# Odd mixer of a three-way-split fp32 transformer step: narrower weight splits, and rotation, gate prelude and first attention scores placed among the projections

## Chip, cores and metric

One core of one Trainium2 chip runs the whole program. The metric is the device time in microseconds of one execution (one core, so this core's time), and the median over repeated executions.

## The reference, cut to what is computed

The program is a stack of layers on 512 tokens of width 1024, all in float32: an even mixer, cross attention, SwiGLU, then the **odd mixer**, cross attention, SwiGLU and two further layers (gated delta rule with a long convolution, with SwiGLU on both sides). The change touches the odd mixer, and the weight splits of every SwiGLU's down projection. The odd mixer is:

```
z = h @ w_in
q_m, k_m, v_m, o_m, gates, c_q, c_kv, k_r = split(z)
i_pre, f_pre = gates + bias                      # 4 heads each
hm = mlstm(q_m, k_m, v_m, i_pre, f_pre)          # decays from cumulative log_sigmoid(f_pre)
hm = rmsnorm(sigmoid(o_m) * hm)
q  = rmsnorm(c_q) @ w_uq    # 8 heads: 64 plain + 32 rotated columns
kv = rmsnorm(c_kv) @ w_ukv  # 8 heads: 64 key + 64 value columns
ha = causal_softmax_attention(q_nope, rope(q_rope), k_nope, rope(k_r), v)
out = concat(hm, ha) @ w_out
```

`w_uq` has 384 rows, `w_ukv` 256, every other weight matrix of the mixer 1024.

## The kernel before, in words

**Linear stages.** `schedule()` gives a list of stages. A linear stage is cut into blocks of 256 output columns; a block fills two banks of the PSUM tile `ACC` (pair 0 or 1, alternating with the running block number). Its weights come in units of 128 x 2048 floats: the SP queue loads `RAW` (two slots), ACT casts it to `WH` (L1836, `split_hi`), DVE forms `WL = RAW - WH` (L2340, `split_lo`), and PE runs three matmuls for each 128x128 tile and 512 tokens (L1003 to L1005: high by high, high by low, low by high). A unit of a matrix with 384 or 256 rows fills 768 or 512 of the 2048 columns, and the third unit of a down projection's block 1536; the load brings only those, the casts of ACT and DVE cover all 2048. The load of unit n waits until unit n-2 is split, `split_hi` of n until PE is through with n-2. DVE then evicts the finished block (L2411 scaled, L2419 plain, L2430 for values, L2435 and L2436 for the two halves of a "nope" block, which go to 64 partitions each).

**The odd mixer's order.** Each engine walks the same list and does its own part in program order; semaphores join them. `od_v` (values of the mLSTM), `od_in` (latents, the rotary key and the gate columns, `OZ[:, 0:6]`), `od_rest` (six blocks: queries, keys, output gates of the mLSTM), into which the latents' norm is already woven (`latent_sums` L1213 after block 2, `latent_scales` L1220 after block 4); `latent` casts the normed latents into `HH` (ACT L2042) and `HL` (DVE L2661); then `uq_nope` (2 blocks), `uq_rope` (1), `kv_nope` (2), `kv_v` (2). The first weight unit of `od_out` is split within the second block of `kv_v`.

**Attention (`mla`, L1680, L2250, L2757).** PE rotates the queries (L1684) and the key (L1685) by a matmul with a fixed matrix, and keeps itself busy with `keep_clock` (13 matmuls on ones, L1010) while DVE multiplies by cosine and sine (L2761 to L2770: three operations for the key, then for each half of the queries two products and four sums of 32 partitions). Then for each of 8 heads: scores (L1701, L1702), maxima on DVE (L2779, L2780), exponentials on ACT (L2262), the division on DVE (L2786), transposes on PE (`turn`, L1715), copies on ACT (L2280), the output matmuls (`output`, L1724). PE's order is scores 0, scores 1, turn 0, then for h = 1..7: scores h+1, turn h, output h-1; output 7 last.

**mLSTM (`mlstm`, L1739, L2283, L2812).** A prelude turns the gate columns (L1741), adds the bias and forms log-sigmoid (DVE L2816 to L2823, ACT L2285 and L2287), sums it over time (PE L1747), turns the results to rows (L1752, L1753), takes the running maximum on 4 partitions (DVE L2830 to L2833) and turns its floor back (L1758); ACT takes the sigmoid of the output gates (L2288) and an exponential (L2290). `keep_clock` stands in it twice (16 and 10 matmuls). Then per head: broadcasts of the row (`head`, L1765 to L1767), decays on ACT (L2297, L2299), scores (L1772, causal tiles of 512, 384, 256 and 128 columns), weights on DVE (L2866), sums and numerators on PE (L1782, L1787). The next head's `head` waits for the decays of the one before.

`BRIDGE` (L39) names the stages that PE opens with some matmuls on ones.

Of the kernel before, what the change touches and what calls it, by code (L numbers as in the profile page):

```python
# [20 lines left out]
P = 128  # L21
S = 512
# [16 lines left out]
BRIDGE = {"ev_out": 6, "xk0": 9, "xq0": 6, "uq_nope": 7, "xk1": 9, "xq1": 6, "b0f2_gu": 8, "b1f2_gu": 8}  # L39
# [50 lines left out]
def schedule():  # L90
# [7 lines left out]
               linear("uq_nope", 2, 3, out="nope", dest="QM"), linear("uq_rope", 1, 3, out="fm", dest="QR", whole=True),  # L98
# [335 lines left out]
def build(nc, wall, xT, memT, params, consts, pos, poolw, params2, consts2, feats, decays, mats, filters, out):  # L434
# [7 lines left out]
    with ctx:  # L442
# [46 lines left out]
        SQB = place("SQB", [P, 2, S], at=(nc.sbuf_usable_end - 4 * S) // 32 * 32 - 4 * S)  # L489
        low = (top[0] + 255) // 256 * 256  # L490
# [39 lines left out]
        MS = place("MS", [P, 3, TC], at=put.at[0] + 4 * 2 * S)  # L530
        COS = place("COS", [P, S], at=put.at[0])
# [6 lines left out]
        LG = put("LG", [P, TC, 8])  # L538
        LT = put("LT", [P, 4, 16])
        LA = put("LA", [P, TC, 4])  # L540
        LF = put("LF", [P, TC, 4])
        LL = put("LL", [P, TC, 4])
        LR = put("LR", [4, 4, S])
        LN = put("LN", [P, 8, 16])
# [5 lines left out]
        ident = CON[:, ccol["ident"][0]:ccol["ident"][0] + P]  # L550
        mask = CON[:, ccol["mask"][0]:ccol["mask"][0] + P]
# [170 lines left out]
        ml_scale = sem("ml_scale")  # L722

# [39 lines left out]

        cell_h0 = [st.h0 for st in stages if st.kind == "mlstm"][0]
        after_cells = [st.b0 for st in stages if st.name == "od_out"][0]

        def cell_columns(k, heads):

            return LN[:, k, :].rearrange("p (c h) -> p c h", c=TC)[:, :, heads[0]:heads[-1] + 1]
# [10 lines left out]
        def causal_scores(h):  # L780

            one, two = 2 * (h % 2), 2 * (h % 2) + 1
            return [ACC[:, two, 384:512], MIX[:, 2, 0:256], ACC[:, two, 0:384], ACC[:, one, :]]
# [216 lines left out]
        def _(pe):  # L1000
# [11 lines left out]
            def pe_linear(st):  # L1012
# [4 lines left out]
                def period(i):  # L1017
# [8 lines left out]
                    for j in in_period(st, i):  # L1026
# [4 lines left out]
                        if not (isinstance(i, int) and b < 2):  # L1031
                            pe.wait_ge(block_done, b - 1)
                        for q in range(st.upb):
# [25 lines left out]
                            elif tcs:  # L1059
                                for tc in range(tcs):  # L1060
                                    if second_block and tc == 2:
                                        late_scale(st.norm)
                                    for k in ks:
                                        if tc == 0 and not st.whole:
                                            pe.wait_ge(h_ready, st.hin + k + 1)
                                        o = ACC[:, 2 * pair:2 * pair + 2, :].rearrange("p a (b n) -> p (a b) n", b=2)[:, tc]
# [149 lines left out]

            def latent_scales():
                pe.wait_ge(diag_ready, latent.nrm + 1)
                for part in range(2):
                    mm = pe.matmul(MIX[:, 1 + part, :], ONES[:], T[:, part, :], start=True, stop=True)  # L1220
                mm.then_inc(scale_ready, 1)
# [458 lines left out]
            def pe_mla(st):  # L1680

                pe.wait_ge(block_done, st.b0)
                for m in range(2):
                    pe.matmul(MIX[:, m, :], rot, QR[:, m, :], start=True, stop=True).then_inc(rotated, 1)  # L1684
                pe.matmul(MIX[0:32, 2, :], rot[0:32, 0:32], OZ[0:32, 5, :], start=True, stop=True).then_inc(rotated, 1)  # L1685
                keep_clock(ACC[:, 0, :], 13)

                def scores(h):
                    if h == 0:
                        pe.wait_ge(rope_done, 2)  # L1690
                        pe.wait_ge(rope_act, 2)
                    if h == 4:
                        pe.wait_ge(rope_done, 3)
                    if h >= 2:
                        pe.wait_ge(ma_exp, h - 1)
                    for tc in (3, 2, 0, 1):
                        n = P * (tc + 1)
                        if tc == 1 and h:
                            pe.wait_ge(ma_freed, h)
                        to = causal_scores(h)[tc]  # L1700
                        pe.matmul(to, QM[:, h, tc * P:tc * P + P], KM[:, h, 0:n], start=True, stop=False)  # L1701
                        mm = pe.matmul(to[:, n - P:n], ident, mask, start=False, stop=True)  # L1702
                        if tc < 2:
                            mm.then_inc(ma_scores, 1)

                def turn(h):
                    pe.wait_ge(ma_probs, h + 1)
                    if h:
                        pe.wait_ge(ma_copied, 3 * h)
                    for kcs in ((0,), (1, 3), (2,)):  # L1710
# [7 lines left out]
                def output(h):  # L1718
                    pe.wait_ge(ma_copied, 3 * h + 3)
                    if h >= 2 and h % 2 == 0:  # L1720
                        pe.wait_ge(t_ready, st.h0 + h // 2)
                    rows = slice(64 * (h % 2), 64 * (h % 2) + 64)
# [16 lines left out]
            def pe_mlstm(st):  # L1739
                for tc in range(TC):  # L1740
                    mm = pe.transpose(MIX[:, 0, 8 * tc:8 * tc + 8], OZ[32:40, 5, tc * P:tc * P + P], ident[32:40, 32:40])  # L1741
                mm.then_inc(ml_columns, 1)
                keep_clock(ACC[:, 0, :], 16)
                pe.wait_ge(ml_gates, 2)
                for j in range(TC):
# [1504 lines left out]
```

## Time and profile before

| | |
|---|---|
| executions (us) | 3825.82, 3818.0, 3819.69; median 3819.69 |
| profiled execution | span 3823.0 us from the first to the last instruction; its device time is not listed apart from the three |
| PE busy | 3710.3 us, 97% |
| DVE / ACT / GpSimd busy | 2048.9 (54%) / 1089.4 (28%) / 69.4 (2%) us |
| mean granted clock of TensorE | 0.987 |
| odd mixer | about 640 to 945 us of the span |

Of the three executions none is marked as the profiled one; the span is 3.3 us over the median. "PE busy" counts a matmul from its start to its modelled end, so matmuls that follow each other closely overlap in it: the start of the next one tells more than a duration. An idle stretch has behind it what released it. The granted clock is the share of the full TensorE clock that the chip gave in a stretch (1.00 is 2.4 GHz, 0.50 is 1.2 GHz).

### The profile page before, as it was taken

To read this page: it belongs to the slowest core of one execution; us is meant where nothing else is said; L and a number is where in the kernel's file an instruction comes from. 1 tells how busy PE (TensorE), PEld (TensorE's weight loads), DVE (VectorE), ACT (ScalarE), POOL (GpSimd) and SP (SyncE) were. 2 spreads that over 40 slices of the span, in tenths; PEclk is the share of its full clock that TensorE was granted. 3 is DMA by queue.
4 is the path that set the end of the run, shared out by engine and by line. 5 is a ranking of instruction groups with operands and counts; after the bars stand their busy time and mean duration, and the time that the engine had idled before them with its cause. 6 is when DMAs were issued, how large, how long until landed. Compare 5 with 4: busy or idle time off the path is not lost.

```text
span 3823.0 us, 43694 instructions
## 1 busy us (share of the span) xinstructions
PE 3710.3 (97%) x17964; PEld 3007.1 (79%) x17964; DVE 2048.9 (54%) x2527; ACT 1089.4 (28%) x1199; POOL 69.4 (2%) x80
## 2 busy tenths in 40 slices
PE   9999999989999999999999999999999998999998
PEld 8878888856778887888876678888888875778887
DVE  6564434563654445443766764434443766665443
ACT  3342222242432222222343222222222343322221
POOL 0000000000000000000110000000000102000000
PEclk9999999999999999999999999999999999999999
DMA  4212222110222222222412222222222413122221
GB/s 150 100 66 99 96 94 99 62 39 24 88 95 99 96 92 94 92 94 105 141 37 94 80 83 93 99 95 95 95 96 92 147 60 100 67 77 88 99 94 72
DMA packets 67766, 343.04 MB, mean 90 GB/s; under 512 B 23748, under 2 KB 23748, under 8 KB 32048
## 3 DMA queue, kind: packets, MB, share of 16 engines
q1 hardware_dynamic: 61872, 303.25, 22.4%
q0 software_dynamic: 5760, 37.86, 2.6%
q8 instruction: 101, 1.65, 0.2%
q14 instruction: 33, 0.27, 0.0%
HBM read 324.31 MB, written 16.78 MB: 89 GB/s over the span
## 4 chain that ended last, share of the span: by engine, by line
PE 88%; DVE 8%; ACT 2%; issue 1%; DMA 0%; SPq 0%; DVEq 0%; ACTq 0%
PE ACC L1003 26%; PE ACC L1004 25%; PE ACC L1005 25%; PE ACC L1669 1%; PE ACC L1497 1%; PE MIX L1497 1%; DVE WL L2340 1%; DVE PT L3172 0%; DVE PT L3170 0%; PE MIX L1724 0%; PE ACC L1411 0%; PE MIX L1462 0%; PE ACC L1010 0%; PE MIX L1423 0%; PE ACC L1657 0%
## 5 line engine op out<-in xcount | busy, mean ns | idle before, releaser
L1003 PE MATMUL ACC<-HH,WH 128*128 128x512 f32 (+1 forms) x3322 | 1305.6, 393 | 18.9 <-DVE X L2439 5.3
L1004 PE MATMUL ACC<-HL,WH 128*128 128x512 f32 (+1 forms) x3322 | 1290.4, 388 | 0.0
L1005 PE MATMUL ACC<-HH,WL 128*128 128x512 f32 (+1 forms) x3322 | 1290.4, 388 | 0.0
L2340 DVE TENSOR_TENSOR WL<-RAW,WH 128x2048 fp32r<-128x2048 f32 x291 | 667.4, 2293 | 445.7 <-ACT WH L1836 445.2
L1003 PEld LDWEIGHTS ACC<-HH,WH 128*128 128x128 f32 x3322 | 625.7, 188 | 165.0 <-issue 17.7
L1004 PEld LDWEIGHTS ACC<-HL,WH 128*128 128x128 f32 x3322 | 625.7, 188 | 130.3 <-issue 5.0
L1005 PEld LDWEIGHTS ACC<-HH,WL 128*128 128x128 f32 x3322 | 625.7, 188 | 128.5
L1836 ACT ACTIVATE WH<-RAW 128x2048 fp32r<-128x2048 f32 x291 | 554.7, 1907 | 599.3 <-PE ACC L1005 591.0
L2449 DVE TENSOR_TENSOR SG<-ACC,RS 128x512 f32<-128x512 f32 x132 | 91.3, 692 | 626.8 <-PE ACC L1005 626.6
L1005 PE MATMUL ACC<-HIDH,WL 128*128 128x512 f32 x1056 | 411.3, 389 | 0.0
L1004 PE MATMUL ACC<-HIDL,WH 128*128 128x512 f32 x1056 | 411.3, 389 | 0.0
L1003 PE MATMUL ACC<-HIDH,WH 128*128 128x512 f32 x1056 | 411.2, 389 | 0.0
L1874 ACT ACTIVATE SG<-SG 128x512 f32<-128x512 f32 x132 | 83.6, 633 | 1071.0 <-DVE SG L2449 1071.0
L1005 PEld LDWEIGHTS ACC<-HIDH,WL 128*128 128x128 f32 x1056 | 198.3, 188 | 41.2
L1004 PEld LDWEIGHTS ACC<-HIDL,WH 128*128 128x128 f32 x1056 | 198.3, 188 | 41.0
L1003 PEld LDWEIGHTS ACC<-HIDH,WH 128*128 128x128 f32 x1056 | 198.3, 188 | 41.0
L2439 DVE SCALAR_TENSOR_TENSOR X<-ACC,X 128x1024 f32<-128x1024 f32 x48 | 58.6, 1224 | 162.1 <-PE ACC L1005 162.1
L1921 ACT ACTIVATE HH<-X,PAR 128x512 fp32r<-128x512 f32 x88 | 57.1, 712 | 157.6 <-DVE X L2439 139.1
L2455 DVE TENSOR_TENSOR T<-T,SG 128x512 f32<-128x512 f32 x132 | 91.5, 693 | 16.8 <-ACT SG L1874 2.1
L2458 DVE TENSOR_TENSOR HIDL<-T,HIDH 128x512 f32 (+1 forms) x132 | 91.4, 692 | 15.2
L2452 DVE TENSOR_TENSOR T<-ACC,RS 128x512 f32<-128x512 f32 x132 | 89.9, 681 | 0.0
L1669 PE MATMUL ACC<-INV,ZS 128*128 128x256 f32 x256 | 63.6, 412 | 17.2 <-DVE ZS L3176 17.2
(529 smaller groups left out, 2907.2 us busy)
## 6 DMA issues: line engine op xcount, KB each, us to landing
RAW<-wall SPq DMA_DIRECT2D x260, 1024.0 KB, 4.7
RAW<-wall SPq DMA_DIRECT2D x24, 768.0 KB, 4.1
KR<-spectra POOLq DMA_DIRECT2D x4, 2048.0 KB, 9.0
x_kept<-X POOLq DMA_DIRECT2D x2, 2048.0 KB, 6.8
FWK<-mats POOLq DMA_DIRECT2D x4, 1024.0 KB, 5.5
spectra<-SQ POOLq DMA_DIRECT2D x8, 512.0 KB, 3.0
spectra<-T POOLq DMA_DIRECT2D x8, 512.0 KB, 3.4
X<-x_kept POOLq DMA_DIRECT2D x2, 2048.0 KB, 14.5
```

The costliest lines, as they stand in the source:

```text
L1003: pe.matmul(out_ap, wh, hh, start=first, stop=False)
L1004: pe.matmul(out_ap, wh, hl, start=False, stop=False)
L1005: return pe.matmul(out_ap, wl, hh, start=False, stop=last)
L1497: mm = pe.matmul(bank[:, 2 * cs + p, :], FWK[:, cs, p, kc, fc * P:fc * P + P], src, start=(kc == 0), stop=(kc == 1))
L1669: mm = pe.matmul(ACC[:, m, 256 * p:256 * p + 256], ZS[:, fc, 2 * p + cs, m * P:m * P + P], INV[:, cs, p, fc, :], start=(fc == cs == p == 0 ...
L1836: act.activation(WH[n % 2][:], RAW[n % 2][:], ACT.Copy).then_inc(w_hi, 1)
L1874: act.activation(SG[:], SG[:], ACT.Silu).then_inc(silu_ready, 1)
L2340: v.tensor_tensor(WL[n % 2][:], RAW[n % 2][:], WH[n % 2][:], ALU.subtract).then_inc(w_lo, 1)
L2449: v.tensor_tensor(SG[:], two[:, 0, :], scale, ALU.mult).then_inc(gate_ready, 1)
L2452: v.tensor_tensor(T[:, j, :], two[:, 1, :], scale, ALU.mult).then_inc(block_done, 1)
L2455: step(v.tensor_tensor(T[:, j, :], T[:, j, :], SG[:], ALU.mult))
L2458: v.tensor_tensor(HIDL[:, bass.ds(off, 1), :], T[:, j:j + 1, :], HIDH[:, bass.ds(off, 1), :], ALU.subtract).then_inc(hid_ready, 1)
```

## The change

- `split_hi` and `split_lo` cover `unit_cols` columns: 768 for `uq_*`, 512 for `kv_*`, 1536 for the third unit of each down block, 2048 for all others.
- `uq_rope` goes ahead of `uq_nope`, and the bridge of 7 goes with it. `uq_nope` gets `whole` (one wait for all latents at its start); `uq_rope` waits chunk by chunk.
- `keep_clock` is taken out of `mla` (13) and of `mlstm` (16 and 10).
- The gate prelude stands in `od_rest`: columns and key rotation on PE after block 0; magnitudes (DVE) after block 1; softplus (ACT) and the key's rotary sum (DVE) with block 2; logs (DVE) and sums (PE) after block 3; differences (DVE) and rows (PE) after block 4; maxima (DVE) after block 5's eviction. The floors (PE) follow `uq_rope`.
- The rotary key is written in place and copied to all heads by ACT in `od_rest`'s block 4. The queries' rotation (PE) follows block 0 of `uq_nope`; its products and sums stand on DVE in `uq_nope`, `kv_nope` and `kv_v`.
- The second half of each "nope" eviction moves from DVE to ACT (`copy_nope`). The sigmoid of the output gates stands on ACT in `uq_nope`.
- `kv_v` accumulates in banks 0 and 1 of `MIX`. Head 0's scores (PE) follow its first block, head 0's maxima (DVE) stand in its second. The split of `od_out`'s first unit on DVE moves from there into `mla`, after head 1's maxima.
- The mLSTM's first head forms two of its four score tiles (512 and 384 columns) in `mla`, ahead of turn 7.

```diff
-BRIDGE = {..., "uq_nope": 7, ...}
+CELL_EARLY = (0, 1)
+BRIDGE = {..., "uq_rope": 7, ...}
...
-               linear("uq_nope", 2, 3, out="nope", dest="QM"), linear("uq_rope", 1, 3, out="fm", dest="QR", whole=True),
+               linear("uq_rope", 1, 3, out="fm", dest="QR"), linear("uq_nope", 2, 3, out="nope", dest="QM", whole=True),
...
+        unit_cols = [TILES * P if st.bpu == 2 or st.kc >= 8 * (j % st.upb + 1) else (st.kc - 8 * (j % st.upb)) * 256
+                     for st in stages if st.kind == "linear" for j in range(st.nu)]
...
+                        if st.name == "kv_v":
+                            pe.wait_ge(rope_done, 3)
+                            if j:
+                                pe.wait_ge(block_done, b)
+                        elif not (isinstance(i, int) and b < 2):
                             pe.wait_ge(block_done, b - 1)
+                        if st.name != "kv_v" and isinstance(b, int) and b - 2 in nope_at:
+                            pe.wait_ge(nope_half, nope_at[b - 2] + 1)
...
-                        if st.name == "od_rest" and (i, j) == (1, 0):
-                            latent_sums()
-                        if st.name == "od_rest" and (i, j) == (2, 0):
-                            latent_scales()
+                        if st.name == "od_rest":
+                            if (i, j) == (0, 0):
+                                gate_columns()
+                                key_rotated()
+                            if (i, j) == (1, 0):
+                                latent_sums()
+                            if (i, j) == (1, 1):
+                                gate_sums()
+                            if (i, j) == (2, 0):
+                                latent_scales()
+                                gate_rows()
+                        if st.name == "uq_rope":
+                            gate_floors()
+                        if st.name == "uq_nope" and j == 0:
+                            queries_rotated()
+                        if st.name == "kv_v" and j == 0:
+                            causal_products(0)
...
-                keep_clock(ACC[:, 0, :], 13)
...
-                scores(0)
-                scores(1)
+                causal_products(1)
                 turn(0)
                 for h in range(1, 8):
                     if h < 7:
-                        scores(h + 1)
+                        causal_products(h + 1)
+                    else:
+                        pe.wait_ge(ma_exp, 7)
+                        cell_products(0, CELL_EARLY)
                     turn(h)
                     output(h - 1)
...
+                cols = columns_of(n, add)
+                act.activation(WH[n % 2][:, 0:cols], RAW[n % 2][:, 0:cols], ACT.Copy).then_inc(w_hi, 1)
...
+                        if isinstance(b, int) and b - 1 in nope_at:
+                            copy_nope(nope_at[b - 1])
+                        if st.name == "uq_nope" and j == 0:
+                            act.wait_ge(block_done, queries_b0)
+                            act.activation(OZ[:, 14:18, :], OZ[:, 14:18, :], ACT.Sigmoid).then_inc(ml_acts, 1)
...
             def act_mla(st):
+                act.wait_ge(ml_columns, 4)
+                act.activation(LN0[:], MIX[:, 3, 0:16], ACT.Exp).then_inc(ml_acts, 1)
...
+                        if st.name == "uq_nope" and j == 1:
+                            query_products(0)
+                            query_sums(0, range(4))
+                        if st.name == "kv_nope" and j == 0:
+                            query_products(1)
+                        if st.name == "kv_nope" and j == 1:
+                            query_sums(1, (0, 1))
+                        if st.name == "kv_v" and j == 1:
+                            query_sums(1, (2, 3))
+                            causal_maximum(0)
...
                             if st.name == "od_rest" and (i, j) == (1, 1):
+                                gate_logs()
                                 latent_diagonals()
                             if st.name == "od_rest" and (i, j) == (2, 0):
+                                gate_differences()
                                 latent_scaled()
+                            if st.name == "od_rest" and (i, j) == (2, 1):
+                                gate_maxima()
...
-                            v.tensor_copy(dst[:, :, 0, :], two[0:64])
-                            v.tensor_copy(dst[:, :, 1, :], two[64:128]).then_inc(block_done, 1)
+                            v.tensor_copy(dst[:, :, 0, :], two[0:64]).then_inc(block_done, 1)
...
+            def gate_maxima():
+                v.wait_ge(ml_columns, 3)
+                v.tensor_copy(LR[:, 0, :], MIX[0:4, 3, :])
+                step(v.tensor_copy(LR[:, 1, :], MIX[0:4, 0, :]))
+                step(v.tensor_tensor_scan(LR[:, 2, :], LR[:, 0, :], LR[:, 0, :], 0.0, ALU.max, ALU.max))
+                step(v.scalar_tensor_tensor(LR[:, 3, :], LR[:, 1, :], -1.0, LR[:, 2, :], ALU.mult, ALU.subtract))
+                v.tensor_scalar(LR[:, 2, :], LR[:, 2, :], -1.0, None, ALU.mult).then_inc(ml_gates, 1)
...
                     if h < 7:
-                        maximum(h + 1)
+                        causal_maximum(h + 1)
+                    if h == 0:
+                        split_lo(st.next_unit, 0, 0)
```

## Rows read from the trace of the kernel before

**Rows 1.** The page's chain that ended last: shares of the span by engine.

```profile
PE 88%; DVE 8%; ACT 2%; issue 1%; DMA 0%; SPq 0%; DVEq 0%; ACTq 0%
```

**Rows 2.** Chain of waits, 640 to 945 us: start, us, what, instructions.

```profile
752.07 1.82 ACT WH L1836
753.91 2.29 DVE WL L2340
...
774.21 4.82 DMA RAW<-wall
...
802.41 1.28 ACT L2262
...
807.42 2.49 PE MIX L1715 x10
...
865.11 0.70 DVE T L2793
...
869.63 2.41 PE MIX L1747 x20
...
877.80 1.12 PE MIX L1765 x2
...
884.69 1.05 PE MIX L1765 x2
```

**Rows 3.** Stretches of the projections: us, busy PE, PEld, DVE, ACT, POOL, clock, DMA.

```profile
749.30:751.20 1.90, 1.58 (x15) 1.39 (x13) 1.85 (x3) 1.85 (x4) 0.00 (x0) 1.00 0.00 0
751.20:765.50 14.30, 13.09 (x54) 9.91 (x54) 13.95 (x13) 6.68 (x6) 0.00 (x0) 1.00 0.10 37
765.50:774.00 8.50, 5.97 (x24) 4.36 (x24) 7.91 (x5) 4.88 (x3) 0.00 (x0) 1.00 0.20 64
774.00:784.40 10.40, 6.22 (x48) 5.87 (x48) 9.41 (x7) 2.61 (x2) 0.00 (x0) 1.00 0.64 208
```

**Rows 4.** Timeline of DVE: start, us, instructions, idle before.

```profile
749.35 1.22 DVE L2411 TENSOR_TENSOR OZ<-ACC,VM 128x1024 f32<-128x1024 f32 x1 [5.35 <-PE ACC L1005]
750.50 3.09 DVE L2661 TENSOR_TENSOR HL<-OZ,HH 128x512 fp32r<-128x512 f32 x5
...
756.12 1.21 DVE L2435 COPY QM<-ACC 64x1024 f32<-64x1024 f32 x1
...
792.99 2.78 DVE L2770 TENSOR_TENSOR QM<-T 32x512 f32<-32x512 f32 x4
...
800.06 1.61 DVE L2779 TENSOR_REDUCE MS<-ACC 128x1 f32<-128x512 f32 x3
...
873.45 1.21 DVE L2830 COPY LR<-MIX 4x1024 f32<-4x1024 f32 x1 [1.13 <-PE MIX L1753]
```

**Rows 5.** Timeline of PE at the projections' start and in the gate prelude.

```profile
751.23 0.50 PE L1003 MATMUL ACC<-HH,WH 128*128 128x512 f32 x1 [0.35 <-DVE HL L2661]
...
877.13 0.40 PE L1758 MATMUL MIX<-CON,LR 4*128 4x4 f32 x4 [1.48 <-DVE LR L2833]
```

**Rows 6.** Timeline of PE in the attention: heads 2 and 3, and the last two.

```profile
818.17 1.13 PE L1701 MATMUL ACC<-KM,QM 96*128 96x512 f32 x2
...
821.33 1.04 PE L1715 MATMUL MIX<-CON,MP 128*128 128x128 f32 x8
...
828.44 1.04 PE L1715 MATMUL MIX<-CON,MP 128*128 128x128 f32 x8
...
855.47 1.09 PE L1715 MATMUL MIX<-CON,MP 128*128 128x128 f32 x8 [1.68 <-DVE MP L2786]
...
858.56 6.51 PE L1724 MATMUL MIX<-OZ,VM 128*64 128x512 f32 x16
```

**Rows 7.** Two stretches with the clock lowered (columns as rows 3).

```profile
785.00:792.00 7.00, 7.00 (x19) 3.48 (x18) 2.50 (x4) 0.47 (x1) 0.00 (x0) 0.52 0.31 130
...
857.00:864.00 7.00, 6.06 (x14) 2.38 (x15) 0.00 (x0) 1.76 (x4) 0.00 (x0) 0.51 0.02 4
```

**Rows 8.** Timeline of ACT: the last decay of the mLSTM's head 0.

```profile
882.71 0.40 ACT L2297 ACTIVATE LE<-MIX,LA 128x128 f32<-128x128 f32 x1
```

More of the change, by code:

```diff
@@ L537, in build @@
         LU = put("LU", [P, 4, S])
[L538 to L544, printed above, removed]
+        lr_at = put.at[0] + 576
+        LRT = place("LRT", [P, 4, S], at=lr_at)
+        LR = LRT[96:100]
+        LN = place("LN", [P, 8, 16], at=lr_at + 4 * 4 * S)
+        LG = place("LG", [P, TC, 8], at=MS_END)
         POSI = place("POSI", [P, S], mybir.dt.int32, at=low)
@@ L762, in unit_of, with columns_of, banks_of @@
             return st.u0 + j, i * (2 * st.upb)
+        values_b0 = [st.b0 for st in stages if st.name == "kv_v"][0]
+        rest_b0 = [st.b0 for st in stages if st.name == "od_rest"][0]
+        queries_b0 = [st.b0 for st in stages if st.name == "uq_rope"][0]
+        nope_blocks = [(st, j) for st in stages if st.out == "nope" for j in range(st.nb)]
+        nope_at = {st.b0 + j: k for k, (st, j) in enumerate(nope_blocks)}
+        unit_cols = [TILES * P if st.bpu == 2 or st.kc >= 8 * (j % st.upb + 1) else (st.kc - 8 * (j % st.upb)) * 256
+                     for st in stages if st.kind == "linear" for j in range(st.nu)]
+        def columns_of(n, add):
+            k = n + add if isinstance(add, int) else n
+            return unit_cols[k] if k < n_units else TILES * P
+        def banks_of(st, j):
+            if st.name == "kv_v":
+                return MIX[:, 0:2, :]
+            pair = (st.b0 + j) % 2
+            return ACC[:, 2 * pair:2 * pair + 2, :]
         cell_h0 = [st.h0 for st in stages if st.kind == "mlstm"][0]
@@ L1215, in latent_sums, with gate_columns, key_rotated, gate_sums @@
                 mm.then_inc(sq_used, 1)
+            def gate_columns():
+                pe.wait_ge(block_done, rest_b0)
+                for tc in range(TC):
+                    mm = pe.transpose(MIX[:, 3, 8 * tc:8 * tc + 8], OZ[32:40, 5, tc * P:tc * P + P], ident[32:40, 32:40])
+                mm.then_inc(ml_columns, 1)
+            def key_rotated():
+                pe.matmul(MIX[0:32, 2, :], rot[0:32, 0:32], OZ[0:32, 5, :], start=True, stop=True).then_inc(rotated, 1)
+            def gate_sums():
+                pe.wait_ge(ml_gates, 2)
+                for j in range(TC):
+                    for i in range(j + 1):
+                        mm = pe.matmul(MIX[:, 3, 32 + 4 * j:36 + 4 * j], tri if i == j else ONES[:], LL[:, i, :],
+                                       start=(i == 0), stop=(i == j))
+                mm.then_inc(ml_columns, 1)
@@ L1217, in latent_scales, with cell_products @@
+            def cell_products(h, kcs):
+                for kc in kcs:
+                    a, n = COFF[kc], S - kc * P
+                    mm = pe.matmul(ACC[:, a // S, a % S:a % S + n], OZ[:, 10 + h, kc * P:kc * P + P],
+                                   OZ[:, 6 + h, kc * P:S], start=True, stop=True)
+                return mm
             def latent_scales():
                 pe.wait_ge(diag_ready, latent.nrm + 1)
+                pe.wait_ge(rope_done, 1)
                 for part in range(2):
@@ L2344, in dve_linear @@
                 n0 = step.n + st.opens
+                own = st.out == "even" or st.name in ("od_rest", "uq_rope", "uq_nope", "kv_nope", "kv_v")
                 scale = RS_OD if st.name[:3] == "od_" else RS[:]
@@ L2358, in period @@
                 def period(i):
-                    if not (st.opens and isinstance(i, int) and i == 0) and st.out != "even" and st.name != "od_rest":
+                    if not (st.opens and isinstance(i, int) and i == 0) and not own:
                         step.n = i * per + n0
@@ L2491, in dve_linear @@
                 periods(v, st, period)
-                if st.out != "even" and st.name != "od_rest":
+                if not own:
                     step.n = n0 + per * st.nb // (2 * st.bpu)
```

226 lines of the change are left out of this document (122 added, 104 removed).

## The prediction

> **What bounds the kernel now.** I read the page first: PE is busy for 97% of the span and holds 88% of the chain that ended last [rows 1]. The reader should see that little is to be had in most stages, and look for the places where the chain leaves PE. The chain of waits does so in one long place, the odd mixer [rows 2]: from 752 us on it steps through ACT's cast and DVE's subtraction of a unit, a load, DVE, an ACT table load, and after 865.1 through the gate prelude until the mLSTM's first head starts at 877.8. The stretches [rows 3] give the size: in 751.2 to 784.4 PE has 13.09 + 5.97 + 6.22 = 25.3 us of matmuls in 33.2 us, while DVE is busy for 31.3 us. So DVE bounds those projections: each block takes a subtraction of 2.29 and two half evictions of 1.21 [rows 2, 4], 4.7 us beside some 4.3 or 3.0 us of matmuls. All else below is counted from E, the end of `od_rest` on PE, 749.3 before.
>
> **Part 1, additions inside `od_rest`.** Here PE is dense, so what is put in costs its full time. Columns: 4 small transposes, 0.4 (as L1758 [rows 5]). (All rows here are of the full clock.) Key rotation: one fp32 matmul of 512 columns, which the trace shows as two records, 1.0 (L1765, 1.05 [rows 2]). Gate sums: 2.4 (L1747 [rows 2]), and a new wait: they need DVE's logs, which DVE does only after it has evicted the same block, 1.2 for the eviction (L2411 [rows 4]) and about 0.3 for a tiny operation and the semaphores: 1.5 of idle PE. Queued behind it on PE is only block 4. Rows: 8 transposes of 0.1, 0.9; their wait for the differences is covered by the latents' scales, which run in that time. Four returns to the big matmuls, about 0.2 each by the first matmul's 0.50 [rows 5] against 0.39 in mid-stream and the wait ahead of it: 0.7. Sum **+6.9**. What DVE (key: three operations of 0.7; magnitudes, logs, differences) and ACT (softplus, key to eight heads) get here lies in gaps of several us per block of 11 us and costs nothing; the next unit's split is the one that would be late, and has about 7 us.
>
> **Part 2, E to turn 0 (807.42 - 749.3 = 58.1 before [rows 2]).** DVE evicts the last block (1.2), and then the maxima come first: before, the 1024-column copy, the scan and two more took the 3.7 from 873.45 to PE's release at 877.13 [rows 4, 5]; with two copies of 0.7 in place of one of 1.2, 3.8. Only then comes the first `HL` (0.6 [rows 4]). So PE starts at E + 5.7 in place of E + 1.9 (751.23 [rows 5]); the bridge covers 1.6 of it [rows 3], and PE stands still for 4 us. From there PE's stream at full clock: 25.3 of projections [rows 3], floors 0.4, queries' rotation 1.9, scores of heads 0 and 1 at 3.2 each (818.17 to 821.33 [rows 6]): 34.0, to **E + 39.7**, all behind one another.
> Is DVE now inside that? A split of 512 columns is bounded by 0.6 (an `HL` chunk, same form [rows 4]) and 2.29; linear between them, 0.7, and 1.0 for 768 columns. Its list from E: eviction and maxima 5.0, `HL` 3.1, splits 1.0 + 1.0 + 0.7 x 4, evictions 7 x 1.2, products 2.8, sums 5.6 (2.78 for four [rows 4]), head 0's maxima 2.3 (800.06 to the table load at 802.41 [rows 2, 4]): 32.0 of 39.7. Block by block, DVE ends the split for `kv_v`'s first block some 0.3 us before PE asks: cover, but thin. Head 0 itself: by the same list its maxima end near E + 34.5; exponentials and division took 3.7 (end of the load, 803.7, to 807.42 [rows 2]), here 4.3 with the last eviction between: E + 38.8, just under PE. ACT's new half evictions are bounded by 0.6 and 1.8 (a cast of 2048 [rows 2]), nearest 1.1 for 1024 columns, and hide beside matmuls of 3 to 4 us. SP: `od_out`'s first unit is loaded once `kv_v`'s first is split, E + 26, lands at E + 31 (4.8 [rows 2]); ACT's cast of it, 1.9, stands ahead of the first exponential, and ends at E + 33: hidden by 1.5. DVE's part of it moves into head 0 of the loop.
> The clock: before, PE's pauses here were followed by 7 us at a granted 0.52 [rows 7], that is, at 1.2 GHz. The 4 us pause after E will do the same; matmuls bound by PE lose half of it, **+3.4** (bounds 0 and 6.8 for two such stretches). Turn 0 at E + 43.1: **-15.0**.
> The table load in the chain (1.28 [rows 2]) counts for nothing now: an Exp of 16 columns brings it ahead of the maxima, from E + 33.0 to 34.3. The Trainium skill (ScalarE: Activation LUTs, "Table sets: the hidden batching unit") puts a load at about 2.7 us and asks that functions of one set be done together; the change does the reverse and spreads Exp, Ln, Sigmoid and Exp over four stages. By that figure the first exponential would begin 1.2 later, turn 0 would come 0.3 after PE is free, and the gain would be 0.3 smaller; the trace's 1.28 stands against it.
>
> **Part 3, the loop of heads.** 7.11 per head (821.33 to 828.44 [rows 6]), PE-bound, unchanged. The split of 2.29 now in head 0 stands between head 1's maxima and division, beside the exponentials on ACT, which take about as long: 0 to 1 us; the old first turns ran at half clock (2.49 for ten small transposes [rows 2]) and lost as much. Net 0. At the end PE stood idle for 1.68 before turn 7, and the stretch after it was at 0.51 [rows 6, 7]: the last two outputs took 6.5, of which some 5 in that stretch, so 2 to 2.6 were lost to it. The early mLSTM tiles (896 of 1280 columns, 1.5 us) fill that idle time. If it keeps the clock, **-2.1** (bounds 0 and 2.5).
>
> **Part 4, mLSTM.** Before, from the last output (865.1) to the second head's broadcasts (884.69) [rows 2]: 19.6. Now: broadcasts of head 0, 2.9 (877.80 to about 880.8), then ACT's decays, which ended at 883.1 [rows 8], 2.3 later: head 1 starts at +5.2. The rest of its tiles (384 columns, 0.7) lies beside them. **-14.4** (the fillers go with the waits they stood in).
>
> **Part 5, elsewhere.** The third unit of down blocks (24 of them) is split 0.5 us faster on DVE and ACT; each has a whole unit of matmuls (over 8 us) as cover before and after: 0.
>
> **Sum:** +6.9 - 15.0 - 2.1 - 14.4 = -24.6. Against the profiled span 3823.0 that is 3798.4; against the median, 3.3 below the span, **3795**. No change would mean within 7.6 us (0.2%), about what a measurement of this kernel can tell.
>
> **Rivals.**
> *A, the clock takes more.* The 1.5 us wait in `od_rest` followed by gate sums that are almost all weight loading brings a lowered stretch of its own, the loop's end keeps its one, and DVE's thin cover in `kv_v` costs 1 us: 3.4 + 2.1 + 2 = 7.5 worse, 3803. For it: a lowered stretch followed each of the marked pauses. Against: the pauses between the `kv` blocks, 4.2 of 10.4 us in the last of the stretches, left the clock at 1.00 there [rows 3].
> *B, the clock takes less.* The 4 us pause shows no lowered stretch (the 1.9 after E before, partly bridged, was followed by none [rows 3]), and the mLSTM's start runs clean: 3790.
> *C, the early attention doesn't come early.* DVE's list, in program order, has the queries' sums between split and eviction of a block; if each of the last four blocks then waits for DVE, turn 0 comes at about E + 52, and the gain shrinks to 16; if the mLSTM also waits for ACT, whose hand is full, it ends within 0.2%: 3812. Against: 7 us of slack in that list.
> *D, slower.* Without the 13 fillers the attention loop starts from a lowered clock, and its many short matmuls don't raise it: a head's 7.1 us are nearly all matmuls [rows 6], at half rate near 13.8. One head so costs 6.7; four (25 / 6.7) eat the gain, all eight (54 - 25) give 3849. It decides at turn 0. For it: the old loop's first transposes ran slow (2.49 for ten [rows 2], 1.04 for eight later [rows 6]). Against: by head 3 they didn't.
> That the change doesn't do what it says is part of C.
>
> **How the numbers follow.** Forecast 0.56 (own range 3790 to 3800), A 0.20, B 0.14, C 0.07, D 0.03. The range holds forecast, A and B with the bounds of the clock's terms: 3786 to 3807; left out are D, most of C and the tails, about 0.15. Faster by over 0.2%: forecast, A, B and half of C, 0.93; within 0.2%: 0.04; slower: 0.03.
>
> **What would show it.** Right: after `od_rest` PE pauses 4 us behind DVE L2830-like copies on 4 partitions, with a lowered clock in the first `uq` blocks; seven projection blocks at some 3 to 4.5 us apart; turn 0 41 to 45 us after E; 7.1 per head; head 1 of the mLSTM 5 us after output 7; `od_rest` 7 us longer, with 1.5 idle before the gate sums. Wrong: `WL` still a releaser between `kv` blocks; first turn waiting for MP by more than 1 us; a loop of over 7.3 per head; a lowered clock for more than three stretches of the mixer.

## The result, and the profile after

| | before | after |
|---|---|---|
| median of the executions on one chip (us) | 3819.39 (3818.0 to 3825.82, 4) | 3795.47 (3795.13 to 3795.8, 4) |
| profiled execution: span | 3823.0 | 3793.7 (device time 3795.61) |
| PE busy | 3710.3 | 3691.3 |
| DVE busy | 2048.9 | 2020.2 |
| ACT busy | 1089.4 | 1074.7 |

The ratio is 0.9932, with a 95% interval of 0.9918 to 0.9946: 23.9 us faster. The span of the profiled execution fell by more, 29.3 us, and where the 5 us between the two come from is a part of what follows.

The page's chain by engine has hardly moved [rows 1]; a change of 0.6% doesn't show there:

```profile
PE 89%; DVE 8%; ACT 2%; issue 1%; DMA 0%; SPq 0%; DVEq 0%; ACTq 0%
```

The chain of waits through the mixer, from the latents' sums to the mLSTM's second head, in the changed kernel (start, us, what, instructions; the counterpart of [rows 2], cut by dots):

```profile
714.96 1.68 PE MIX L1259 x16
727.75 1.10 issue
729.08 2.40 PE MIX L1276 x20
...
757.68 1.23 DVE OZ L2510
758.94 0.68 DVE LRT L2760
...
762.69 0.70 DVE HL L2793
763.43 0.79 PE ACC L1030
773.89 1.22 DVE QM L2541
775.11 0.60 DVE WL L2426
...
795.48 1.28 DVE MP L2929 x4
796.79 0.70 DVE MS L2921
...
850.96 1.05 PE MIX L1834 x2
...
856.24 1.12 PE MIX L1834 x2
```

The load, the cast and the table load that stood in it before are gone. Two new things stand in it: the gate sums at 729.08 behind a wait, and the gate maxima (L2760 onward) between `od_rest`'s last eviction and the first `HL`. From 773.89 to 792.8 all of its pieces but a short one are DVE's, and DVE's division ends at 796.75, where PE's turn 0 begins. The last prelude is no longer there: `head` starts as the last output ends.

The windows of the same kernel (columns as in [rows 3]; `od_rest` ends at 757.5, turn 0 stands at 796.85):

```profile
757.50:763.40 5.90, 1.71 (x15) 1.52 (x13) 5.55 (x8) 3.44 (x6) 0.00 (x0) 0.97 0.00 0
763.40:796.90 33.50, 33.47 (x167) 27.06 (x168) 26.81 (x41) 15.85 (x22) 0.00 (x0) 0.95 0.27 95
796.90:844.20 47.30, 44.31 (x221) 27.90 (x219) 29.12 (x75) 25.79 (x79) 0.00 (x0) 1.00 0.07 23
844.20:850.90 6.70, 5.32 (x28) 2.87 (x27) 1.26 (x2) 1.98 (x4) 0.00 (x0) 1.00 0.01 1
```

In 757.5 to 763.4 DVE is busy for 5.55 of the 5.9 us and PE for 1.71; behind that PE has no idle time before turn 0 (33.47 of 33.50), and the clock of 0.95 is one stretch of lowered clock at its start:

```profile
763.40:767.00 3.60, 3.57 (x9) 2.85 (x10) 3.31 (x6) 0.00 (x0) 0.00 (x0) 0.58 0.02 5
767.00:769.20 2.20, 2.20 (x11) 1.57 (x10) 0.00 (x0) 0.00 (x0) 0.00 (x0) 1.00 0.32 110
```

PE's timeline (start, us, instructions, idle before; the counterpart of [rows 5, 6]) has what was added, three waits, and what the clock did behind the first:

```profile
691.59 0.41 PE L1266 MATMUL MIX<-CON,OZ 8*128 8x8 f32 x4
691.92 1.04 PE L1270 MATMUL MIX<-OZ,CON 32*32 32x512 f32 x2
...
729.08 0.39 PE L1276 MATMUL MIX<-CON 128*128 128x4 f32 x2 [1.40 <-DVE CON L2749]
...
731.88 0.40 PE L1032 MATMUL ACC<-HH,WL 128*128 128x512 f32 x1
...
733.20 0.63 PE L1030 MATMUL ACC<-HH,WH 128*128 128x512 f32 x1
...
763.43 0.79 PE L1030 MATMUL ACC<-HH,WH 128*128 128x512 f32 x1 [4.22 <-DVE HL L2793]
...
802.88 1.09 PE L1802 MATMUL MIX<-CON,MP 128*128 128x128 f32 x8 [1.23 <-DVE MP L2929]
```

The same form of matmul takes 0.40 at 731.88 and 0.63 at 733.20, and follows its neighbour by 0.43 instead of 0.23: that is a stretch at half clock (a lowered stretch from here on), 3.4 us long. It begins at 732.3, about 1 us behind the gate sums, with PE at work since the wait of 1.40 ended. Half of its length, 1.7 us, is the most that such a stretch can cost.

DVE's timeline has the two waits between `od_rest` and `kv_nope`, which matter below as its slack:

```profile
769.25 1.22 DVE L2525 COPY QR<-ACC 128x1024 f32<-128x1024 f32 x1 [2.53 <-PE ACC L1032]
...
773.89 1.22 DVE L2541 COPY QM<-ACC 64x1024 f32<-64x1024 f32 x1 [2.56 <-PE ACC L1032]
```

To compare executions I cut the mixer at eight events on PE: first of the latents' sums (S), end of `od_rest` (E, where the matmuls on ones begin), first matmul of the `uq` stages (U), turn 0 (T0), turn 7 (T7), first broadcasts of the mLSTM's heads 0 and 1 (H0, H1), first matmul of `od_out` behind the mLSTM's last numerators (M). Each figure is the difference of two starts in PE's timeline of that profiled execution, in us; "rest" is the span less S to M.

| execution | S-E | E-U | U-T0 | T0-T7 | T7-H0 | H0-H1 | H1-M | S-M | rest |
|---|---|---|---|---|---|---|---|---|---|
| before | 36.3 | 2.1 | 56.2 | 48.1 | 22.3 | 6.8 | 40.1 | 211.9 | 3611.1 |
| x1, before again | 36.3 | 2.1 | 55.3 | 47.5 | 20.3 | 5.4 | 40.1 | 207.0 | 3610.5 |
| after | 42.7 | 5.9 | 33.4 | 47.3 | 6.7 | 5.4 | 40.1 | 181.6 | 3612.1 |
| x0, after again | 42.6 | 6.0 | 34.8 | 47.4 | 6.7 | 5.4 | 41.8 | 184.6 | 3610.0 |
| x2 | 42.7 | 6.0 | 42.4 | 47.4 | 6.7 | 5.4 | 40.1 | 190.6 | 3605.2 |
| x3 | 36.3 | 2.1 | 52.6 | 48.2 | 22.4 | 6.8 | 40.1 | 208.5 | 3609.4 |
| x4 | 42.6 | 6.0 | 39.9 | 47.4 | 6.7 | 5.4 | 40.1 | 188.0 | 3614.3 |
| x5 | 42.7 | 6.0 | 33.6 | 47.3 | 6.7 | 5.4 | 40.1 | 181.7 | 3615.6 |
| x6 | 44.3 | 6.0 | 32.5 | 47.4 | 6.7 | 5.4 | 38.4 | 180.6 | 3613.3 |
| x8 | 42.6 | 2.1 | 33.3 | 47.4 | 6.7 | 5.4 | 40.1 | 177.5 | 3605.0 |
| x9 | 39.4 | 6.0 | 33.5 | 47.4 | 6.7 | 5.4 | 40.1 | 178.3 | 3610.3 |
| x10 | 41.1 | 2.1 | 33.2 | 47.3 | 6.7 | 5.4 | 40.1 | 175.9 | 3609.6 |

The table repeats within 0.2 us wherever the code is the same and no lowered stretch has moved, which is why the small questions below are decided in it. The rest spreads over 10 us, though little in it was edited: the down splits, and the 1.4 us that the changed kernel adds ahead of S. Medians of four or five executions so carry an error of some us.

### The profile page after: what moved, and what is told of

Its sections match the earlier page's. It is cut to its first block, busy times and chain, and to the rows that moved or that the text cites. A ratio compares the mean times of both kernels' runs of the same rounds, so it can differ in the third digit from the quotient of the medians.

```text
span 3793.7 us, 43545 instructions
## 1 busy us (share of the span) xinstructions
PE 3691.3 (97%) x17886; PEld 2993.2 (79%) x17886; DVE 2020.2 (53%) x2524; ACT 1074.7 (28%) x1203; POOL 69.5 (2%) x80
## 4 chain that ended last, share of the span: by engine, by line
PE 89%; DVE 8%; ACT 2%; issue 1%; DMA 0%; SPq 0%; DVEq 0%; ACTq 0%
PE ACC L1030 26%; PE ACC L1032 26%; PE ACC L1031 26%; PE ACC L1778 1%; PE ACC L1606 1%; PE MIX L1606 1%; DVE PT L3295 0%; DVE PT L3293 0%; PE ACC L1520 0%; PE ACC L1037 0%; PE MIX L1571 0%; PE MIX L1813 0%; PE MIX L1532 0%; PE ACC L1766 0%; PE MIX L1407 0%
## 5 line engine op out<-in xcount | busy, mean ns | idle before, releaser
L2426 DVE TENSOR_TENSOR WL<-RAW,WH 128x2048 fp32r<-128x2048 f32 (+3 forms) x291 | 642.5, 2208 | 455.1 <-ACT WH L1902 454.4
L1902 ACT ACTIVATE WH<-RAW 128x2048 fp32r<-128x2048 f32 (+3 forms) x291 | 536.1, 1843 | 608.6 <-PE ACC L1032 601.2
L1032 PEld LDWEIGHTS ACC<-HIDH,WL 128*128 128x128 f32 x1056 | 198.2, 188 | 41.1
```

The costliest lines, as they stand in the source:

```text
L1032: return pe.matmul(out_ap, wl, hh, start=False, stop=last)
L1902: act.activation(WH[n % 2][:, 0:cols], RAW[n % 2][:, 0:cols], ACT.Copy).then_inc(w_hi, 1)
L2426: v.tensor_tensor(WL[n % 2][:, 0:cols], RAW[n % 2][:, 0:cols], WH[n % 2][:, 0:cols], ALU.subtract).then_inc(w_lo, 1)
```

## The experiments

**x1: the kernel before, once more.** No edit.

> The kernel before, profiled once more. Open is why the two profiled spans differ by 29.3 us and the medians by 23.9. Theory C (the clock's lowered stretches fall differently from execution to execution, and the first profiled one of before was a costly one): its device time is 3818 to 3820, its span 5 to 7 us under 3823.0, and what is missing are lowered stretches of the clock somewhere in the program. Rival (the change costs something outside the odd mixer that its profile happened not to show): this one's span is again near 3823.

Measured 3819.22 us (one execution), span 3817.5: 5.5 below the first profiled one, and S to M 4.9 below. The difference sits in four places of the table, U-T0 0.9, T0-T7 0.5, T7-H0 2.0 and H0-H1 1.5, and each holds a lowered stretch that x1 lacks or has shorter: between S and M the clock was lowered for 27.3 us in the first execution and for 17.1 here, and half of the 10.2 between them is 5.1. Here, at the end of the attention, the clock stayed up, and the last outputs took 3.93 instead of 6.51 [rows 6]:

```profile
851.06 1.09 PE L1715 MATMUL MIX<-CON,MP 128*128 128x128 f32 x8 [1.67 <-DVE MP L2786]
...
853.90 3.93 PE L1724 MATMUL MIX<-OZ,VM 128*64 128x512 f32 x16
```

```profile
855.00:862.00 7.00, 6.94 (x50) 5.31 (x48) 2.26 (x5) 2.31 (x4) 0.00 (x0) 1.00 0.00 0
```

The same wait of 1.7 stands in front of turn 7 in both executions, and only in one did a lowered stretch follow. So the slow end of the attention in [rows 7] is no fixed property of the kernel, and against this execution the changed one gains 25.4 in S to M, less some 1.4 that it adds ahead of S: 24.0, as the medians of the first measurement say (23.9). But x1 is itself a short execution. The thirteen others of the kernel before that ran beside it have a median of 3825.85 (3819.4 to 3829.85), the seven beside x5, x6, x8 and x9 one of 3824.03, and the nine beside x10 and x0 one of 3823.3: elsewhere the first profiled execution, not x1, is the usual one.

**x2: `uq` and `kv` splits cover 2048 columns again**, all else as changed.

```diff
-        unit_cols = [TILES * P if st.bpu == 2 or
+        unit_cols = [TILES * P if st.out != "resid" or st.bpu == 2 or
```

> The changed kernel with the casts of the uq and kv units over all 2048 columns again (the down units stay narrow). Theory P (PE is the bound of this phase now, and DVE stands just under it): DVE gets 2 x 1.3 + 4 x 1.6 = 9.0 us more, its idle time of 2.5 us in each of the first two blocks takes the first two, the rest comes to the path: +5 to +6.5 us against the changed kernel's 3795.5. Rival (the gain came from the moved work alone, casts are hidden): 0 to +1. Rival 2 (DVE is already the bound everywhere): +9.

Measured 3799.74 (3797.65 to 3807.81, 4), 4.3 above the changed kernel's first median; U-T0 is 9.0 longer. PE now waits in `kv_nope`, and a lowered stretch of 6.8 us begins within that wait, at 782.5 (PE's timeline, then a window):

```profile
784.02 0.77 PE L1030 MATMUL ACC<-HH,WH 128*128 128x512 f32 x1 [3.90 <-DVE WL L2426]
...
802.46 1.09 PE L1802 MATMUL MIX<-CON,MP 128*128 128x128 f32 x8 [0.76 <-DVE MP L2929]
```

```profile
783.00:795.00 12.00, 10.82 (x49) 8.79 (x50) 11.54 (x11) 4.55 (x4) 0.00 (x0) 0.74 0.33 115
```

A wide split is 1.34 longer than one of 768 columns (2.29 against 0.95) and 1.61 longer than one of 512 (0.68). The three and four of them are 10.5 us of DVE. On PE they come out as waits of 4.7 (3.90 and 0.76 above); another part goes into DVE's idle time ahead of its first two evictions, 5.1 us in the changed kernel (2.53 and 2.56) and 2.6 here. What is left of the 9.0 is the clock's: between U and T0 it was lowered for 12.2 us here and for 3.0 in the changed kernel, 4.6 us of time at half rate. Against x0, where the stretch behind the pause was as long as here (6.8), the loss is 7.6. So the wide splits cost some 5 us of waiting, as expected, and whether the further clock loss comes with them every time stays open. The median lost less than the stage says; how much of that is the rest of the program, which in the profiled execution was short (3605.2), four executions don't settle.

**x3: narrow splits alone, in the kernel before** (`unit_cols` in its `split_hi` and `split_lo`, down units too, nothing moved).

> The kernel before with only the narrow casts (uq, kv and the third unit of each down block). Theory P: the DVE-bound blocks become bound by PE or by their evictions; the load, cast and split of od_out's first unit ahead of the last eviction stay: -6 to -6.5 us against 3819.4 (3813). Rival (that chain of load and casts holds the end, nothing is gained): 0 to -2. Rival 2 (the down units' splits were on the path as well, 24 x 0.5 us): -18.

Measured 3822.09 (3818.58 to 3825.0, 10 executions) beside 3825.85 of the kernel before, ratio 0.9991 (0.9981 to 1.0): hardly anything. U-T0 is 2.7 shorter than in x1 and 3.6 shorter than in the first execution, not the 6 or more expected. From U to the queries' rotation (L1684 before, L1692 here) it is 28.6 against 33.3 in both others, 4.7 shorter; behind that 1.0 to 2.0 are lost again. Its chain of waits shows what keeps the projections from getting shorter still:

```profile
764.69 1.22 DVE KM L2445
765.92 1.23 DVE KM L2446
767.15 0.61 DVE WL L2350
767.82 4.70 DMA RAW<-wall
772.54 1.92 ACT WH L1845
774.49 2.29 DVE WL L2350
776.78 1.14 DVE VM L2440
777.97 3.78 PE MIX L1692 x4
```

DVE needs only 0.61 for `kv_v`'s split, but `od_out`'s first unit is loaded behind it, cast and split (4.70 + 1.92 + 2.29), and the last eviction of `kv_v` stands on DVE behind that split. PE waits 3.88 for it, and the queries' rotation runs at a lowered clock (3.78 for four; 1.98 in x1). The clock was lowered for 15.0 us between U and T0 here and for 6.8 in x1, which is enough for the second loss; one profile can't tell whether the narrow splits bring it. At the loop's end this execution again shows the slow outputs of [rows 6], 6.58 for sixteen. The down units are in here too, and the rest is 1.1 us below x1's, within its spread: Part 5 at zero stands.

**x4: both "nope" halves evicted by DVE again** (`copy_nope` and its waits out).

```diff
-                            v.tensor_copy(dst[:, :, 0, :], two[0:64]).then_inc(block_done, 1)
+                            v.tensor_copy(dst[:, :, 0, :], two[0:64])
+                            v.tensor_copy(dst[:, :, 1, :], two[64:128]).then_inc(block_done, 1)
```

> The changed kernel with both halves of the nope evictions on DVE again (ACT's copies taken out). DVE gets 4 x 1.2 = 4.8 us more. Theory P: the first is hidden by an idle time of 2.5 us, the other three come to the path less some 0.5 us of cover: +3 us (2.5 to 4). Rival (PE-bound, thick cover): 0 to +0.5. Rival 2 (DVE-bound throughout): +4.8.

Measured 3804.35 (3803.97 to 3804.78, 4), far more than the 3 us expected; U-T0 is 6.5 longer, for four evictions of 1.2 (4.8) and lowered clock: 6.8 us behind the pause ahead of `uq_rope`, as in x0, and 3.4 more from 784.2 on. Against x0 the loss is 5.1: 2.9 in PE's waits, up to 1.7 in that further stretch, and some 0.5 that I can't place. The waits say whom PE waits for:

```profile
783.75 0.47 PE L1030 MATMUL ACC<-HH,WH 128*128 128x512 f32 x1 [2.01 <-DVE WL L2421]
...
791.93 1.12 PE L1310 MATMUL ACC<-KM,QM 96*128 96x512 f32 x2 [0.69 <-DVE KM L2537]
...
801.39 1.09 PE L1799 MATMUL MIX<-CON,MP 128*128 128x128 f32 x8 [0.20 <-DVE MP L2925]
```

**x5: no early mLSTM tiles** (all four score tiles in the mLSTM).

```diff
-CELL_EARLY = (0, 1)
+CELL_EARLY = ()
...
-                    else:
-                        pe.wait_ge(ma_exp, 7)
-                        cell_products(0, CELL_EARLY)
```

> The changed kernel without the two early mLSTM tiles: PE stands idle for some 1.7 us before turn 7 again, and all four tiles are formed in the first head, beside the decays. Theory K (the tiles' gain was the clock that they kept): the clock falls for a stretch at the last two outputs, which take 5.5 to 6.5 us instead of 3.9: +1.5 to +3 us, and the first head stays hidden beside the decays. Rival (their gain was the work taken out of the first head): outputs as fast as now, but head 1 of the mLSTM 1.5 us later: +1.5, with the clock at 1.00. Rival 2: no effect, within 0.5.

Measured 3796.59 (3790.44 to 3799.39, 4). No stage differs by more than 0.2. The idle time before turn 7 is back, and nothing slow follows:

```profile
844.44 1.09 PE L1802 MATMUL MIX<-CON,MP 128*128 128x128 f32 x8 [1.68 <-DVE MP L2926]
...
847.28 3.93 PE L1813 MATMUL MIX<-OZ,VM 128*64 128x512 f32 x16
```

In this execution the tiles moved forward gain nothing: they fill an idle time that comes anyway, and in `mlstm` they fit beside the decays. Without them the clock fell behind turn 7 in two profiled executions (before, x3) and stayed up in two (x1, x5); with them it stayed up in all eight. So they aren't needed for it, and whether they make it likelier stays open: one execution of x5 can't tell, and the stages ahead differ from those of before.

**x6: the pause before `uq_rope` filled** with 24 matmuls on ones in place of 7.

```diff
-BRIDGE = {..., "uq_rope": 7, ...}
+BRIDGE = {..., "uq_rope": 24, ...}
```

> The changed kernel with a bridge of 24 instead of 7 matmuls on ones ahead of uq_rope, so that PE has something to do in the 4.2 us in which it waits for the first HL behind the maxima. Theory K: the lowered stretch at 763 to 766.7 us (3.4 us) goes, and as PE is the bound there, 1.7 us of time with it: -1 to -1.7. Rival (DVE's list is the bound, faster matmuls only wait longer): 0. Rival 2 (the fillers outlast the wait): +0.3 to +1.

Measured 3798.45 (3795.98 to 3801.32, 4), so the median shows no gain. PE's timeline:

```profile
757.35 5.52 PE L1037 MATMUL ACC<-ONES 128*128 128x128 f32 x48
763.30 0.50 PE L1030 MATMUL ACC<-HH,WH 128*128 128x512 f32 x1 [0.43 <-DVE HL L2793]
...
795.80 1.09 PE L1802 MATMUL MIX<-CON,MP 128*128 128x128 f32 x8 [0.34 <-DVE MP L2929]
```

No lowered stretch follows before turn 0, and U-T0 falls by 0.9, not by the 1.7 of the stretch: now turn 0 waits 0.34 for DVE's division. With x0, where a stretch of 6.8 us gave 34.8, three lengths have three prices: 0, 3.4 and 6.8 us lowered give 32.5, 33.4 and 34.8. The first 3.4 us are half covered by DVE. What was won here was lost in `od_rest` (44.3), where the lowered stretch behind the gate sums was 6.8 us long instead of 3.4.

**x8: gate maxima behind `uq_rope`'s eviction** instead of ahead of the first `HL`; the floors follow in `uq_nope`.

```diff
-                            if st.name == "od_rest" and (i, j) == (2, 1):
-                                gate_maxima()
...
+                            if st.name == "uq_rope":
+                                gate_maxima()
...
-                        if st.name == "uq_rope":
-                            gate_floors()
                         if st.name == "uq_nope" and j == 0:
+                            gate_floors()
                             queries_rotated()
```

> The changed kernel with the running maxima (five DVE operations, 3.8 us) after the eviction of uq_rope instead of ahead of the first HL; the floors follow block 0 of uq_nope on PE. No work is added or taken. Theory Q (in-order DVE: these 3.8 us stand on the path only because nothing covers them there): PE starts uq_rope 3.8 us sooner and the lowered stretch behind the pause goes (1.7), but PE waits some 0.7 us for the maxima before the rotation: -3.5 to -5. Rival (DVE is the bound from there on, and its list is as long as before): 0 to -1.

Measured 3788.52 (3784.55 to 3790.93, 4), ratio 0.991 (0.9893 to 0.9928), 7.0 below the changed kernel's first median, of which S to M explains 4.1. E-U is back at 2.1, U-T0 doesn't grow:

```profile
755.97 0.50 PE L1030 MATMUL ACC<-HH,WH 128*128 128x512 f32 x1 [0.35 <-DVE HL L2792]
...
765.45 0.41 PE L1289 MATMUL MIX<-CON,LRT 4*128 4x4 f32 x4 [0.98 <-DVE LRT L2763]
```

The maxima cost PE 3.9 us at the old place and a wait of 0.98 at the new one, and DVE takes them in an idle time that it had anyway: it waits 2.53 for `uq_rope` and 2.56 for `uq_nope` in the changed kernel, 1.17 and nothing here. The lowered stretch behind the pause is gone too; x6, which lost it alone, has 32.5 in U-T0, so the maxima still cost 0.8 of that where they stand now.

**x9: gate sums beside the latents' scales**, a block later, behind the split and the eviction that they had to wait for.

```diff
-                            if (i, j) == (1, 1):
-                                gate_sums()
                             if (i, j) == (2, 0):
+                                gate_sums()
                                 latent_scales()
```

> The changed kernel with the gate sums on PE after block 4 of od_rest, ahead of the latents' scales, instead of after block 3. No work is added or taken. Theory K: the wait of 1.4 us for DVE's logs goes, and with it the lowered stretch of 3.4 us that followed it (1.7 us at the big matmuls): -2.5 to -3.3. Rival 1 (the stretch came from the sums themselves, which are almost all weight loading, and moves with them): -1.4 only. Rival 2 (the differences now wait and delay the latents): 0.

Measured 3792.41 (3790.63 to 3798.19, 4), ratio 0.9924 (0.9904 to 0.9943). S-E is 3.3 shorter: the wait of 1.40 is gone, the lowered stretch behind the sums too (1.7), and one return to the big matmuls (0.2).

**x10 and x0: both moves together, and the changed kernel again**, five executions of each on one chip.

> Both moves together: the gate maxima behind uq_rope's eviction and the gate sums beside the latents' scales, all else as in the changed kernel. Theory K (the two places cost what the single runs showed, and the savings are independent): od_rest ends 39.4 us after the latents' sums (changed kernel 42.7), the first uq matmul stands 2.1 us after that end (5.9), from there to turn 0 33.3 to 33.5, everything behind it unchanged; latents' sums to the mixer's output 174.3 us against 181.6, median about 3787, and 7 us under the changed kernel on this chip. Rival S (they share one saving: the lowered clock in uq comes back once od_rest ends sooner, or DVE now meets the maxima, its split for kv_v and head 0 in a denser list): only 4 us, 177.5, median near 3791. Rival N: the spread of executions is as wide as the difference, and only the stages tell it.

> The changed kernel, unaltered, for its own spread. Theory C (part of the gain seen between two profiled executions is which lowered-clock stretches each fell into): its executions spread over about 8 to 12 us as those of the kernel before do, the median lies at 3795 to 3800, the profiled execution's stages in the mixer differ from the first one's only where a lowered stretch begins or is gone (each by 1.7 us or a multiple), and the total of lowered clock moves with the span at half its length. Rival: the placement is fixed by the program; then the stages repeat within 0.1 us and the executions within 1 us, as the four of the first measurement did.

x10: 3789.21 (3786.74 to 3790.97), ratio 0.9912 (0.9899 to 0.9926). x0: 3795.08 (3792.23 to 3796.84), ratio 0.9925 (0.9912 to 0.9939). The five executions of the one all lie below the five of the other, 5.9 us between the medians. In the table x10 stands 5.7 below "after", 1.6 short of the sum of the two moves, and all of that in S-E, which is 41.1 and not 39.4. The four matmuls of the latents' scales behind the sums tell why; first x9, then x10, PE's timeline:

```profile
742.41 1.96 PE L1328 MATMUL MIX<-T,ONES 128*128 128x512 f32 x4
```

```profile
737.22 3.26 PE L1327 MATMUL MIX<-T,ONES 128*128 128x512 f32 x4
```

The code and what stands ahead of it on PE are the same in both, PE had no idle time, and still a lowered stretch began there in one execution (granted 0.50 from 738 to 741) and not in the other. So the move takes away the wait in both executions and the stretch only in one. x0 lies 28.2 under that same median, where the first measurement gave 23.9. Its five executions spread over 4.6 us, wider than its first four (0.7) and narrower than I had put it, and between its two profiled ones only U-T0 (1.3) and H1-M (1.7) differ. x10 is faster than both kernels: it lies 34 us under the median of the one before on the same chip (3823.3), 28 to 39 by the interval.

## Why the prediction was right, and where it wasn't

The 3795 hit the median, 3795.47, and that it hit so closely is luck: the sum was 3798.4 for a span that measured 3793.7, and the 3.3 taken off for the median should have been 1.8 put on. The two errors, 4.7 and 5.1, cancel.

- **The reference point.** I took the profiled span, 3823.0, as 3.3 above the median. Later executions show 1.7 to 2.1 us between span and device time, so that execution took some 3825, the slowest of those shown, near 6 above their median; x1 has 10.2 us less of lowered clock in the mixer, and half of that is its 4.9 to within 0.2. The step that failed is reading [rows 7] as what the kernel's pauses always bring. Against x1 the change is worth 24.0 in the mixer; against the profiled execution 28.9. Which of the two is the usual gain stays open: the first medians say 23.9, those beside x0 28.2, and three of the four medians of the kernel before lie nearer to the first profiled execution than to x1.
- **Part 1, +6.9: measured about 7.8.** Columns and key rotation ahead of S took 1.4 as put, S-E grew by 6.4. The wait was 1.40 (put at 1.5), the sums 2.4. What was not in the sum is the lowered stretch behind them, up to 1.7; I had it in rival A. The rows and returns then come to about 0.9 (6.4 less 1.4, 2.4 and 1.7), less than the 1.6 put for them. x9, with neither wait nor stretch, is 3.3 shorter.
- **Part 2, -15.0: measured -18.9 against the profiled execution, -18.0 against x1.** PE's start was right (E + 5.9 against E + 5.7; 4.22 idle against 4). The stream was not: 33.4 in all, where I had put 34.0 and 3.4 more for the clock. Its size came from the busy column of [rows 3], which at each of the seven pauses also counts a last matmul's tail to its modelled end and a slower first one (0.47 to 0.50 for 0.39): a block of 18 matmuls at one every 0.23 is 4.1, of 12 at 0.23 or 24 at 0.12 2.7 to 2.9, in all 23.5 for the seven blocks and not 25.3. The clock took one stretch of 3.4 us in this execution (two lengths in x0), and x6 shows 0.9 of its 1.7 on the path. That term, priced at its doubled length, is the other one mis-sized.
- **The tie of PE and DVE** was right and is what the changed stage hangs on. DVE's list was put at 32.0 us and measured 32.4 (5.55 and 26.81 in the windows above). Head 0's division was put at E + 38.8 and ended at E + 39.3 (796.75), PE's turn stood at E + 39.4. x2, x4 and x6 each move one of the two, and in each PE waits for DVE ahead of turn 0 (0.76, 0.20, 0.34) where it had not. The narrow split measured 0.95 and 0.68, put at 1.0 and 0.7; the half eviction on ACT 1.01, put at 1.1. The table load (1.28) lay where it was put, ahead of the first exponential and beside DVE's maxima; the load of about 2.7 us that the Trainium skill gives (ScalarE: Activation LUTs, "Table sets: the hidden batching unit") appears in none of the runs: here it lies between a cast that ends at 791.46 and an exponential that starts at 792.77.
- **Part 3, -2.1: its mechanism isn't shown.** From turn 7 to the last output's end it is 9.6 in the profiled execution before, 6.8 in x1, which has no early tiles, 6.7 in the changed kernel and in x5. The 2.9 are the clock's, in some executions and not in others; the step that failed is that the tiles save them in each. What T0-T7 gained, 0.7, was lowered clock too: against x1 it is 0.2. PE now waits 1.23 for head 1's division, behind the split moved there, a little over the 0 to 1 us put; it doesn't show because the first turns of x1 had lost 1.7 to a lowered stretch that the changed kernel doesn't have.
- **Part 4, -14.4: right.** From the last output to head 1: 19.6 before, 5.3 after, so -14.3; against x1, with 18.9, it is -13.6. This is read from the stages; no run puts the prelude back alone.
- **Part 5, 0: right** (x3).
- **The rivals.** A's stretch behind the gate sums came true, its others did not. B's reason, a pause with no lowered stretch behind it, didn't come. C and D did not come: `WL` released no block, and the loop ran 7.11 per head at a granted 1.00, the fillers out. Against x1 the parts make +7.8 - 18.0 - 0.3 - 13.6 = -24.1; the spans differ by 23.8.

## What to carry to other kernels

Before pricing a change by the slow stretches in one profile, profile the unchanged kernel twice: what differs between the two can't be put down to the change, and here it was 5 of 29 us. Size a stream of matmuls by the distance from start to start, not by the sum of busy times. When small work moves into a dense stage, its place matters as much as its cost: the gate maxima and sums cost some 6 us more where they were put than one block later, behind what they wait for or where their engine idles anyway. And a split made narrower pays only where the engine that does it is the one waited for: alone it made the projections 4.7 us shorter and the time to turn 0 2.7 to 3.6, and within the reordered stage it saves some 5 us of waiting, 7.6 to 9.0 with the clock.

## What was not expected of the hardware

The lowered stretches of the mixer, at a granted 0.50, were 3.4 us long (the changed kernel), 6.8 (x0) or 10.2 (x3), and where they fall isn't fixed by the program: the same matmuls, with no idle time ahead, were lowered in x10 and not in x9, and the same 1.7 us wait before turn 7 was followed by one in the first execution and in x3, and by none in x1 and x5. In x6, with the pause filled by matmuls on ones, the stretch behind it was gone, which was worth 0.9 us, while another stretch had grown by as much elsewhere; whether the two hang together stays open.
